# The last expert turn reordered: down weights first, gate and up in parts, TensorE weighing the gathered rows, context rows and norms by stream

## What is computed

```python
h2 = rmsnorm(x, norm_ffn_g[layer]) * (1.0 + sc2) + sh2
if last:
    x = x + g2 * hier_moe(h2.reshape(b * s, d), *moe).reshape(x.shape)
else:
    hc2 = rmsnorm(xc, norm_ffn_g[layer]) * (1.0 + csc2) + csh2
    out = hier_moe(jnp.concatenate([h2.reshape(b * s, d), hc2.reshape(-1, d)], axis=0), *moe)
    x = x + g2 * out[: b * s].reshape(x.shape)
    xc = xc + cg2 * out[b * s:].reshape(xc.shape)
```

```python
(jax.nn.silu(xblk @ w_gate[e]) * (xblk @ w_up[e])) @ w_down[e]
```

## Time and profile before

| | us |
|---|---|
| median of 3 runs | 2130.61 (2130.08 to 2130.62) |
| the profiled execution's own time | 2130.71 |
| its span, first to last instruction | 2128.9 |
| PE busy | 1994.3 (94%) |
| DVE, ACT, POOL busy | 871.8, 343.2, 87.5 |
| expert phase of the first layer, near | 985 to 1428 |
| its combination and norm, until L715 runs | 1428 to 1457 |
| last turn of the second layer and the end | 2075 to 2129 |

### The profile page before, as it was taken

How to read it: one execution, slowest core, us unless ns; L and a number is a source line. 1 busy time by engine, 2 the same in 40 slices (tenths; PEclk the granted TensorE clock), 3 DMA queues, 4 the chain that set the end, 5 groups by cost and what they waited for, 6 DMA issues and landing times.

```text
span 2128.9 us, 31500 instructions
## 1 busy us (share of the span) xinstructions
PE 1994.3 (94%) x12745; PEld 1384.4 (65%) x12745; DVE 871.8 (41%) x1876; ACT 343.2 (16%) x696; POOL 87.5 (4%) x91
## 2 busy tenths in 40 slices
PE   8999999999999999999989889999999997779886
PEld 7888888868888888875544455546657453334443
DVE  3388886235855559644211111132562311111112
ACT  2321111321111130320000000012132000000001
POOL 0000000000000010000000001110000000000100
PEclk9999999999999999999998999999999998889998
DMA  8667567334577646347999999994234999999994
GB/s 308 238 241 272 197 237 260 135 119 153 203 290 263 233 156 212 129 159 298 416 425 427 426 424 423 416 414 169 87 151 178 369 412 425 425 423 426 423 420 197
DMA packets 143368, 616.27 MB, mean 289 GB/s; under 512 B 8884, under 2 KB 16108, under 8 KB 113184
## 3 DMA queue, kind: packets, MB, share of 16 engines
q1 hardware_dynamic: 131824, 584.37, 69.4%
q0 software_dynamic: 9568, 26.35, 3.5%
q10 hardware_dynamic: 1872, 4.08, 0.5%
HBM read 593.97 MB, written 27.79 MB: 292 GB/s over the span
## 4 chain that ended last, share of the span: by engine, by line
PE 73%; DMA 18%; DVE 4%; issue 3%; ACT 1%; SPq 1%; DVEq 0%; ACTq 0%
PE T L802 16%; PE T L715 11%; DMA ring<-in_exp_w_down 8%; PE T L821 8%; PE T L956 7%; DMA ring<-in_exp_w_gate 6%; PE T L1021 5%; PE T L971 5%; PE T L941 4%; PE T L1309 3%; DMA ring<-in_exp_w_up 3%; DVE ring L2560 2%; PE T L984 2%; PE T L1207 1%; PE T L1245 1%
## 5 line engine op out<-in xcount | busy, mean ns | idle before, releaser
L802 PE MATMUL T<-X,ring 128*128 128x256 f32 x1536 | 337.6, 379 | 0.7 <-ACT X L1536 0.7
L802 PEld LDWEIGHTS T<-X,ring 128*128 128x128 f32 x1536 | 292.1, 190 | 40.8 <-issue 1.6
L956 PE MATMUL T<-ring,S 128*64 128x512 f32 x1280 | 285.1, 598 | 5.9 <-DMA ring<-in_exp_w_up 5.9
L971 PE MATMUL T<-ring,S 128*32 128x256 f32 x2048 | 148.7, 450 | 81.3 <-issue 80.4
L956 PEld LDWEIGHTS T<-ring,S 128*64 128x64 f32 x1280 | 90.2, 137 | 172.6 <-issue 169.2
L1967 DVE SCALAR_TENSOR_TENSOR S<-ring,cs,S 128x512 f32<-128x512 f32 x280 | 197.9, 746 | 0.6
L941 PE MATMUL T<-S 128*128 128x128 f32 x1536 | 177.7, 276 | 0.7 <-DVE S L2185 0.7
L941 PEld LDWEIGHTS T<-S 128*128 128x128 f32 x1536 | 174.2, 192 | 2.5 <-issue 1.6
L821 PE MATMUL T<-S,ring 128*128 128x256 f32 x768 | 175.2, 381 | 0.0
L971 PEld LDWEIGHTS T<-ring,S 128*32 128x32 f32 x2048 | 75.5, 125 | 148.9 <-issue 116.2
L821 PEld LDWEIGHTS T<-S,ring 128*128 128x128 f32 x768 | 144.8, 190 | 20.5 <-DVE S L2021 0.8
(11 more groups left out here) (383 smaller groups left out, 1866.1 us busy)
## 6 DMA issues: line engine op xcount, KB each, us to landing
ring<-in_exp_w_down SPq DMA_DIRECT2D x61, 2048.0 KB, 20.8
ring<-in_exp_w_gate SPq DMA_DIRECT2D x54, 2048.0 KB, 19.8
ring<-in_exp_w_up SPq DMA_DIRECT2D x54, 2048.0 KB, 24.5
ring<-in_ffn_w_up SPq DMA_DIRECT2D x24, 2048.0 KB, 12.7
ring<-in_mod_w SPq DMA_DIRECT2D x24, 2048.0 KB, 8.0
ring<-in_ffn_w_down SPq DMA_DIRECT2D x12, 2048.0 KB, 11.8
ring<-in_exp_w_gate SPq DMA_DIRECT2D x40, 512.0 KB, 7.7
ring<-in_exp_w_up SPq DMA_DIRECT2D x40, 512.0 KB, 8.6
```

What stands on the lines that cost most here:

```text
L802: ins = pe.matmul(T[:, 2 * (m % 2) + h, 0:S], w[:, k, m * P:(m + 1) * P], x1[:, k, :], start=(k == 0), stop=(k == KT - 1))
L956: ins = pe.matmul(T[c * B:(c + 1) * B, s, :].rearrange("p (g n) -> p g n", g=2), xgT[:, k, s * B:(s + 1) * B], w[:, :, k * CH + c * 256:k ...
L971: ins = pe.matmul(T[32 * f:32 * f + 32, 1, j * 256:(j + 1) * 256] .rearrange("p (g n) -> p g n", g=2), xgT[:, k, row:row + 32], w[:, :, k, ...
```

## The change

- **SP, last turn.** a's down weights come first, after the wait for the previous turn's first `down`. b's gate and up follow, each in four pieces of 512 KB (two feature tiles), counted in `early_came[0..3]`. After the wait for the previous turn's second `down` come b's down weights in three pieces.
- **PE, last turn.** a's hidden transpose, `down` of a, the one-hot transposes, then `up` of b by pieces. In its middle, after two of the four pieces, stand the matmuls on the gathered rows of tile 0; those of tile 1 stand around b's hidden transpose, and `down` of b comes last (f is its tile of 128 hidden features).
- **Weighing on PE.** DVE no longer combines the rows. It makes `by_weight`, for each tile and choice the identity times the token's weight, and PE multiplies g0 and g1 by it (`weighed`). The sums of the main stream lie in banks 7, 6, 0 and 3 (`X_SUMS`).
- **POOL.** The gathers of tiles 2 and 3 (context, l = 0) wait until the first three quarters of b's down have landed.
- **By stream, l = 0.** The main stream is combined and normed first, then the context's rows are weighed; the context's norm lies in the multiplication by `w_in_cd`. `H` has another layout (`H2`), so that each stream is in one piece. Norms after it are counted one higher.

```diff
-        gwT, y_last = part(S1, 0, 512), part(S1, 3072, D)
+        gwT, y_last = part(S2, 2048, 512), part(S1, 3072, D)
+        by_weight = part(S2, 2560, 8, P)
+        sum_sq = (part(S1, 1024, 8, S), part(S2, 0, 8, S))
+        H2 = part(H, 0, 2, 8, S)
...
+        X_SUMS = (7, 6, 0, 3)
+        def x_sum(j):
+            return T[:, X_SUMS[j], :].rearrange("p (a n) -> p a n", a=2)
...
-    gate_up_at(b0, 3, (r["landed"][3], r["landed"][4]))
     down(tl, 0, a0)
-    down(tl, 1, b0)
+    for h in range(4):
+        for j in range(2):
+            src = weights[j][l][ds(b0, 1)].rearrange("e (p k) n -> p (e k) n", p=P)
+            sp_.dma_start(mslot(3 + j)[:, 2 * h:2 * h + 2, :], src[:, 2 * h:2 * h + 2, :])\
+                .then_inc(early_came[h], 16)
+    sp_.wait_ge(r["y_full"], 2 * tl + 2)
+    wd = mslot(5, MJ, D)
+    load_parts(0, 2, b0, wd[:, 0:2, :], early_came[4])
+    load_parts(2, 3, b0, wd[:, 2:3, :], early_came[4])
+    load_parts(3, 4, b0, wd[:, 3:4, :], r["landed"][5])
...
+    def gathered_x(t, tiles):
+        pe.wait_ge(r["cg"][t], 32 * (l + 1))
+        for j in tiles:
+            if t == 0:
+                take(pe, u0[f"comb{l}"] + j)
+            for i in range(2):
+                weighed(t, 2 * j + i, x_sum(j)[:, i, :], t == 0 and i == 0)
     keep_busy(4, 3)
     turn_hidden(tl, 0)
-    up(tl, 1, 3, second, in_front + 2 * PAIRS + 1)
+    down(tl, 0)
     pe.wait_ge(r["gw"], l + 1)
     for t in range(TT[l]):
         ins = pe.transpose(T[:, 3, t * P:(t + 1) * P], onehot[:, t, :], ident)
     ins.then_inc(r["gw_full"], 1)
+    pe.wait_ge(r["xT"], 2 * tl + 3)
+    for h in range(4):
+        pe.wait_ge(early_came[h], 128 * (l + 1))
+        for k in (2 * h, 2 * h + 1):
+            for c in range(2):
+                ins = pe.matmul(T[c * B:(c + 1) * B, 1, :].rearrange("p (g n) -> p g n", g=2),
+                                xgT[:, k, B:2 * B],
+                                ring[:, 3:5, k * CH + c * 256:k * CH + (c + 1) * 256],
+                                start=(k == 0), stop=(k == KT - 1))
+        if h == 1:
+            pe.wait_ge(r["gw_out"], l + 1)
+            pe.wait_ge(r["cb"], l + 1)
+            gathered_x(0, range(4))
+    ins.then_inc(r["m_full"], 1)
+    gathered_x(1, range(2))
     turn_hidden(tl, 1)
-    down(tl, 0)
-    down(tl, 1)
+    gathered_x(1, range(2, 4))
+    pe.wait_ge(early_came[4], 128 * (l + 1))
+    pe.wait_ge(r["m_act"], 2 * tl + 2)
+    pe.wait_ge(r["hT"], 2 * tl + 2)
+    for f in range(MJ):
+        if f == 3:
+            pe.wait_ge(r["landed"][5], 16 * tl + 16)
+        off = (f % 2) * P + (f // 2) * B
+        for n in range(2):
+            ins = pe.matmul(T[n * B:(n + 1) * B, 5, :], hT[:, 1, off:off + B],
+                            mslot(5, MJ, D)[:, f, n * 512:(n + 1) * 512], start=(f == 0), stop=(f == MJ - 1))
+    ins.then_inc(r["y_full"], 1)
+def weighed(t, k, out, start):
+    for j, rows in enumerate((g0, g1)):
+        ins = pe.matmul(out[:, (t % 2) * P:(t % 2 + 1) * P], rows[:, t, k * P:(k + 1) * P],
+                        by_weight[:, 2 * t + j, :], start=(start and j == 0), stop=False,
+                        skip_group_check=True)
+    return ins
...
+def combine_ctx():
+    u = u0["comb0"]
+    for j in range(4):
+        take(pe, u + 4 + j)
+        if (u + j) % 4 in X_SUMS:
+            read(pe, u + X_SUMS.index((u + j) % 4))
+        for i in range(2):
+            from_last(0, 1, 2 * j + i, pair(u + 4 + j)[:, i, :], i == 0)
+    norm_sums(4, n=S, sq=sum_sq[0])
+    keep_busy(3)
+    norm_spread(4, n=S)
+    for t in range(2, 4):
+        pe.wait_ge(r["cg"][t], 32)
...
-combine(0)
-norm(4, sq=S2)
+combine_x(0)
+combine_ctx()
-dense(c, 4, lambda k: H[:, k, 0:S], u, S, ready=(h_ready, 24))
+dense(c, 2, lambda k: Hx[:, k, :], u, S, ready=(h_ready, 24))
+norm_sums(5, n=S, sq=sum_sq[1])
+take(pe, u + 1)
+for m in range(2, 4):
+    for k in range(KT):
+        ins = pe.matmul(pair(u + 1)[:, m - 2, :], slot(c)[:, k, m * P:(m + 1) * P], Hx[:, k, :],
+                        start=(k == 0), stop=(k == KT - 1))
+    if m == 2:
+        pe.wait_ge(n_nrm, 8 * 3 + KT)
+        norm_spread(5, n=S)
+ins.then_inc(full[(u + 1) % 4], 1)
-dense(c + 1, 2, lambda k: H[:, k, :], u + 2, N2)
...
     act.sem_inc(r["y_all"], 1)
-    gate(tl, 1)
     act.wait_ge(r["gw_full"], l + 1)
     A(gwT[:, 0:TT[l] * P], T[:, 3, 0:TT[l] * P], ACT.Copy).then_inc(r["gw_out"], 1)
     act.wait_ge(r["y_full"], 2 * tl + 3)
     for n in range(2):
         ins = A(y_last[0:B, n * 512:(n + 1) * 512], T[n * B:(n + 1) * B, 4, :], ACT.Copy)
     ins.then_inc(r["y_last"], 1)
+    gate(tl, 1)
...
+    for t in range(tt):
+        for j in range(2):
+            ins = V.tensor_scalar(by_weight[:, 2 * t + j, :], ident, rt[:, 740 + 4 * j + t:741 + 4 * j + t],
+                                  None, ALU.mult)
+    ins.then_inc(r["cb"], 1)
     gated(tl, 1)
     hidden(tl, 1)
-def combine(l):
-    tt = TT[l]
-    v3 = lambda off: rt[:, off:off + tt]
-    w1, w2 = v3(740), v3(744)
-    for t in range(tt):
-        dve.wait_ge(r["cg"][t], 32 * (l + 1))
...
-combine(0)
-norm(4, lambda k, v: gsv[:, 2, k, v:v + 1])
+combine(0, 0)
+norm(4, lambda k, v: gsv[:, 2, k, v:v + 1], n=S, out=H2)
+combine(0, 1)
+norm_rs(5, n=S)
+norm_scale(5, lambda k, v: gsv[:, 2, k, v:v + 1], n=S, out=H2, v0=1)
...
+        if t == 2:
+            pool.wait_ge(early_came[4], 128)
```

More of the change, by code:

```diff
@@ new lines, in experts, with from_last @@
+                ins.then_inc(r["y_full"], 1)
[5 more added lines that the diff above has]
+                return ins
+            def from_last(l, v, k, out, start):
+                pe.wait_ge(r["y_last"], 3 * l + 2 + k // 4)
+                return pe.matmul(out, y_last[:, k * P:(k + 1) * P], gwT[:, v * S:(v + 1) * S],
+                                 start=start, stop=False, skip_group_check=True)
@@ L1135, in combine @@
                     for j in range(4):
-                        if v > 0 or j >= 2:
-                            take(pe, u + j)
                         for i in range(2):
-                            out = pair(u + j)[:, i, :]
-                            ins = from_last(v, 2 * j + i, out, v > 0 or j >= 2)
-                            if v > 0 or j >= 2:
-                                ins = gathered(v, 2 * j + i, out)
-                        ins.then_inc(full[(u + j) % 4], 1)
+                            ins = weighed(t, 2 * j + i, pair(u + 4 + j)[:, i, :], False)
@@ L1146, in _ @@
+                        if t == 3:
+                            ins.then_inc(full[(u + j) % 4], 1)
             pe.wait_ge(s_zero, 1)
@@ L1379, in _ @@
             landed(c + 3)
[L1380 removed]
+            dense(c + 3, 1, lambda k: H2[:, :, k, :], u, N2, n=192)
             take(pe, u + 1)
@@ L1509, in _ @@
                 dense(c, 4, lambda k: kt8(oo, k), u0["out_cd"] + 2 * j, S)
-            norm(5, n=S)
+            norm(6, n=S)
             route(1)
             experts(1)
-            combine(1)
-            norm(6, n=S, sq=S2)
+            combine_x(1)
+            norm(7, n=S, sq=sum_sq[0])
         @block.scalar
@@ L1574, in norm_shift @@
                     for v in range(v0, v0 + n // S):
-                        ins = A(out[:, k, v * S:(v + 1) * S], out[:, k, v * S:(v + 1) * S], ACT_F,
-                                bias=modv[:, l, 24 * w + k, v:v + 1])
+                        h = out[:, k, v * S:(v + 1) * S] if out is not H2 else H2[:, v, k, :]
+                        ins = A(h, h, ACT_F, bias=modv[:, l, 24 * w + k, v:v + 1])
                     ins.then_inc(h_ready, 1)
@@ L1855, in _ @@
             experts(0)
-            norm(4, X, sq=S2, wait=lambda k: read(act, u0["comb0"] + 4 + k // 2), shift=(1, 0, 3))
+            norm(4, X, n=S, sq=sum_sq[0], wait=lambda k: read(act, u0["comb0"] + k // 2))
+            norm_shift((1, 0, 3), n=S, out=H2)
+            norm_squares(5, X[:, :, S:N2], n=S, sq=sum_sq[1], wait=lambda k: read(act, u0["comb0"] + 4 + k // 2))
+            norm_root(5, n=S)
+            norm_shift((1, 0, 4), n=S, out=H2, v0=1)
             u = u0["in_cd"]
@@ L1910, in _ @@
             heads_out(15)
-            norm(5, X, n=S, wait=lambda k: read(act, u0["out_cd"] + k // 2), shift=(1, 1, 4), table=ACT.Exp)
+            norm(6, X, n=S, wait=lambda k: read(act, u0["out_cd"] + k // 2), shift=(1, 1, 5), table=ACT.Exp)
             route(1)
             experts(1)
-            norm(6, X, n=S, sq=S2, wait=lambda k: read(act, u0["comb1"] + k // 2))
+            norm(7, X, n=S, sq=sum_sq[0], wait=lambda k: read(act, u0["comb1"] + k // 2))
         @block.vector
@@ L2103, in norm_scale @@
                         v = v0 + j
-                        ins = STT(out=out[:, k, v * S:(v + 1) * S], in0=X[:, k, v * S:(v + 1) * S],
-                                  scalar=gain(k, v), in1=T[:, 6, j * S:(j + 1) * S], op0=ALU.mult, op1=ALU.mult)
+                        h = out[:, k, v * S:(v + 1) * S] if out is not H2 else H2[:, v, k, :]
```

(1 more changed line is left out.)

85 lines of the change are left out of this document (35 added, 50 removed).

## The result

| | before | after |
|---|---|---|
| median, us | 2130.61 | 2144.78 (2144.06 to 2145.68) |
| ratio of after to before, 95% interval | | 1.0058 (1.0046 to 1.0070) |
| profiled execution, its span | 2130.71, 2128.9 | 2144.06, 2142.3 |
| PE busy | 1994.3 | 2005.6 |

The changed kernel is slower by 14 us by the medians and by 12 by the ratio, and outside the range of the prediction. (A fourth execution of the kernel before took 2135.66 us, and on the chips of the later runs its median was 2 to 4 us higher, so the ratio is the better figure.) PE is busy for 11 us more, about what the additional weighing takes; the gain that was to pay for it is taken back by waits.

The account below looks back on a forecast made before the run. PE was taken as the bound (73% of the chain of waits) except in both last turns, where the chain runs through b's up load. 2130.71 - 0.8 (second layer) + 1.15 (first) + 0.4 (wait) = 2131.5 us, range 2126 to 2140.

Parts of the forecast that it names:

- the wait that is added: PE's wait for tile 0's rows inside `up` of b: none in the second layer, 0.4 us in the first.
- The gather's duration: Tile 0's second gather, last turns: between 5.8 and 10.1 us, taken as 8.5.
- The first gather's start: POOL's first gather, second layer: at about 2081.5 on the old clock, not 2087.7.
- The store: Last store ahead of the gathers: between 5.8 and 12.0 us, taken as 5.8.
- PE's arrival: PE reaches the gathered rows in the middle of `up` of b at 1420.6 (first layer) and 2091.85 (second).
- Half late: Slow store or gathers, waits of 2 to 4 us per layer, 2135 to 2142; 0.18 together with norm not hidden.
- another case: First layer: the context's norm waits for something and isn't hidden, up to +6, 2137; 0.18 together with half late.
- Late: Rows as late as before: waits of 7.2 and 4.7 us with clock drops, +15.3, or 2146; chance 0.1.
- signs of being wrong: PE's wait for `g0`, `g1` over 2 us; `down` of b awaiting its last piece; `w_in_cd` starting before 1451 or after 1456.
- The loads themselves: b's weights in pieces, last turns: 6.3 MB cost 0.7 us more, of the stream alone, and this is covered.
- The first layer's multiplication: `w_in_cd`: effective start 1455.75 against 1454.6, +1.15 us, the additional weighing of 7.4 us eating the gain.
- The second layer's stretch: Second layer's last turn: last add at 2110.85 instead of 2111.68, -0.8 us.

Follow-up runs that it names:

- the repetition: The changed kernel itself run once more, with nothing changed: 2147.17 us, ratio 1.0060.
- the run with loads alone: Kernel before with only the new load order and pieces and PE's order to match, DVE combining the rows: 2137.59 us, ratio 1.0022.

## Why the prediction was wrong

**The account of the parts, by medians** of kernels beside which before had 2133.06: the two streams -6.4 (to 2126.67), weighing on PE +10.1 (to 2136.74), loads, order of PE and the wait in `up` +10.4 (to 2147.17, the repetition). By my own terms these were about -6.3, +11.1 and -4.1: the last part alone was wrong, by 14 us, in sign too. It divides further. The wait's place is 7 to 9 us of it (2137.76 with the rows behind `up`). The rest, the new loads with PE's order, is 1 to 2 us where PE weighs (ratio 1.0024 against 1.0017, within the noise) and 5 to 6 where DVE combines (2137.59 against before; 0.9999 against 0.9970): weighing gives PE work while b's weights come. With b's loads left out the kernel stands at 1.0008, 1.3 us above before, where my sum without an added wait gives 0.4: it was the traffic that the sum had wrong.

**The step that failed** is *the wait that is added*: "the second gather 1.3 after that, and it lands after between 5.8 and 10.1; I take 8.5, the first layer's. Result: 2091.3, where 2091.85 is wanted, no wait." Three terms of it:

- *The gather's duration.* Measured 10.65 and 10.56, so my figure was 2.1 too little in each layer; for the second layer its own row had 10.1. The 8.5 was of a gather that ran while the last of b's weights drained. The change makes the gathers earlier and b's weights later, so they meet. I had noticed that for the stores and kept the gathers' figure; in the run without b's loads, where a gather takes 5.5 us, neither layer waits.
- *The first gather's start.* In the second layer I had it at 2081.5 on the old clock, 1 us before the end of `up` of a. It came 1.1 after it (2093.49 against 2092.40). Of these 2 us the last store's duration is 1.0 (6.8 instead of 5.8), its issue 0.6 (2085.41, 2075.5 on the old clock, instead of 2074.9), and 0.4 is that ACT has a's silu ahead of the wait for the stores in its order; that last part could be read from ACT's code.
- *The store.* 6.0 to 7.7 us, where before the four of the second layer took 7.6 to 12.0. The direction and the reason (smaller packets beside it) held; the 5.8 was a little low.

PE's arrival was right: 1422.8 with the opening taken off is 1420.6, as forecast. The mechanism was on the list as *Half late*, waits of 2 to 4 us in each layer, with 2135 to 2142. Its waits came (3.99 and 3.63), with a clock drop in one or both. I gave it 0.18 together with another case and let the range end at 2140, inside the case. My own bounds should have carried the range further: with the gather at its 10.1 and a drop in both layers the sum is 2138, with the store at its 12.0 as well it is past *Late*, 2146. Of the signs of being wrong that I gave, two came: PE's wait for the rows is over 2 us, and the multiplication by `w_in_cd` starts after 1456 (at 1461.72, or 1459.5 without the opening; less the wait beyond forecast and its clock, 5.2, it is 1454.3, where 1453.6 was forecast).

**The loads themselves** were mis-sized: "6.3 MB cost 0.7 us more". From the end of `up` of a to the landing of b's last down piece it is 19.0 us in the second layer of the changed kernel (2092.40 to 2111.42), where it was 16.1 (2082.51 to 2098.62), and 18.3 in the first (1412.53 to 1430.83), where it was 13.5 (1410.46 to 1423.97). With b whole on the new order it is 15.9 and 13.9. So the order costs next to nothing, and the pieces make b's stream 3 to 4.4 us longer (2.4 in the run with b's gate and up alone in pieces). In the changed kernel this doesn't hold PE up by itself: less the wait of 3.63, PE would have wanted b's last piece of up at 2107.5 and its down at 2113.3, and they landed at 2104.69 and 2111.42. But it keeps the weights flowing beside the gathers, and in the run with loads alone it is the waits of 3.0 and 3.2 us. GB/s of a stretch without small transfers beside it, 408 against 428, didn't show it. The Trainium skill (DMA: Bandwidth & Descriptors, Bandwidth) gave, as an estimate, 3.8; the measurements are nearer to it than to my 0.7.

**What was right.** The first layer's multiplication: 1.15 us forecast, with the weighing's 7.4 eating all that the streams bring. Without the wait and its clock it is +1.6 (7.2 less 3.99 and 1.6), and the streams alone bring 5.8 there (6.06 less 0.26 of the opening). The second layer's stretch: -0.8 forecast, 3.4 less the wait of 3.6 is -0.2. The weighing at 0.115 us a record: 10.1 measured of the 11.1 that I had. The hold costs nothing that shows. The context's norm is hidden: from 1461.72 to 1491.39 PE's timeline has no gap in the multiplication by `w_in_cd`. PE waits neither for b's pieces in the changed kernel nor for its down, and by the times above it wouldn't without its wait either.

**What stays open.** Why a gather beside the weights moves its first packet only some 4 us after its issue, and why 6.3 MB in pieces take 3 to 4.4 us longer when a stretch of them runs at 408 against 428 GB/s. And the late turns of the second layer, the same code in all these kernels, vary by 1 to 2 us between them; PE waits there for weights in each, so I count it as the phase of the stream, without a run for it.

## What to carry to other kernels

A transfer's duration belongs to what flows beside it: when a change moves a small transfer earlier and a large load later, price it with both together (here 11 us, not 8.5, and 5.5 without the load). Count packets by queue in a short stretch: while both flow, the small one gets half of them. How long the large one still flows is then half of the question, and pieces make that longer. A wait put into the middle of an in-order engine costs its length and, here more often than not, a stretch at half the clock behind it; with it behind `up`, 7 of the 14 us were gone. And work that an idle engine does (DVE's combining, 0.75 + 1.29 us a tile beside `down`) is dear on the busy one, 1.8 us a tile more; of this change only the part that took no PE time was worth keeping, once DVE's order let it work.

## What the runs showed of the hardware beyond that

The same pause has not always the same price: 3.63 us of waiting left the clock at full (32 records in 3.81 us), while 3.90 in another execution of the same kernel were followed by 6.75 us for these records, and 3.99 by 5.44. A figure from one profile for such a place is good to 3 us. And a gather of 512 KB from scattered 4 KB rows took 5.5 us beside three others like it and no weights, a plain store of 128 KB 3.1 to 3.2 us where only the end of a's down was still flowing (first layer of that run; 4.3 and 6.8 in the second, with more of it to come): half or more of what the kernel sees of either is the other traffic.
